# Row transposes of a fused two-block kernel, each split over two 64-row tiles of TensorE

## The chip, the cores and the metric

One NeuronCore of a Trainium2 chip runs the whole program; the other cores idle. The metric is the device time of one execution in microseconds (us). Three runs of the kernel before gave 3456.67 us as their median (3455.22 to 3461.14). The profile shown here is that of one more execution.

## The reference, cut to what matters

1024 tokens of width 1024, in float32, go through two transformer blocks. The first block mixes (a gated linear recurrence beside latent attention, merged by sigmoid gates and projected), adds the residual, normalizes and sends each token to 2 of 32 experts. The second block mixes (a chunked linear recurrence with 4 heads beside a pooling branch), normalizes, and sends each token to 8 of 64 experts. An expert computes, on the rows that were routed to it:

```python
def block_ffn(args):
    xb, e = args
    return (jax.nn.silu(xb @ w_gate[e]) * (xb @ w_up[e])) @ w_down[e]
```

xb has 1024 columns, w_gate[e] and w_up[e] are 1024 x 256, w_down[e] is 256 x 1024. The results are scaled by the router's share and summed per token.

## The kernel before, in words

TensorE multiplies a stationary operand, loaded by LDWEIGHTS, by a moving one, and contracts over the partitions. So whatever is to be multiplied along its columns must first lie with these columns on partitions. Rows of tokens are turned for that with `nc.tensor.transpose(out, rows, ident)`: the 128 x 128 piece of rows is the stationary operand, the identity is the moving one (128 columns), and the turned piece lands in PSUM, from where VectorE copies it to SBUF. Eight such pieces (C = 8) turn 128 tokens of 1024 columns. All engines run their own lists of instructions; semaphores order them.

Five places of this kind matter here.

- **experts** (run twice: for 32, then for 64 experts). A step works on two blocks of 64 tokens of up to two different experts at once: the two halves (PART = 64) sit on two column tiles of the array (shape 128*64 in the profile), the first with the weights from `w_gu`/`w_dn` (lines 1894, 1919), the second with the staged copies `st_gu`/`st_dn` (lines 1897, 1922). TensorE's list for step i is: 8 gate-and-up products per half into `gu_ps`; `turn_rows(i + 1)`, the 8 transposes of the next step's rows into `x_ps` (line 1883), whose source takes every 8th column of `xb` (`xb[:, slot, c:D:C]`); `finish(i)`, the down products of step i - 1 into `y_ps`; and the 2 transposes of the hidden values into `h_ps` (line 1906), whose source takes every 2nd column of `hid` (`hid[:, slot, c::FC]`). A float32 product is issued as two instructions over the 512 moving columns, a transpose as one. VectorE copies `x_ps` out (line 1978) and `h_ps` (line 1980), makes `hid` (1976) and stages weights (1964, 1971); ScalarE does Silu (1944) and the scaling of `y_ps` (1950); GpSimd gathers rows and scatters sums by indirect DMA; SyncE's queue loads 3 MB of weights for each expert, into one of 5 slots in the first experts and of 4 in the second, and posts `g_ready`/`d_ready` (lines 1771, 1775) once they have landed.
- **merge** (the first block's merging stage) and **mix_out** (the second mix's output). For each of 8 tiles of 128 tokens TensorE runs an output projection (32 instructions of 512 columns, lines 1176 and 2505, shape 128*128), then the turn of the tile before (`turn`, lines 1154 and 2484, 8 contiguous pieces), then the router's products of the tile before that (`route`, lines 1165 and 2495, shape 128*64).
- **take_sums** (the sums of the first experts): for 8 tiles VectorE adds two halves of the sums (line 1306), TensorE turns the tile (line 1293), VectorE copies it out (line 1302).

Of the kernel before, what the change touches and what calls it, by code (L numbers as in the profile page):

```python
# [25 lines left out]
P = 128  # L26
S = 1024
D = 1024
T = S // P
C = D // P  # L30
BANK = 512
# [13 lines left out]
PART = P // 2  # L45
# [69 lines left out]
def begin(nc, A, G, gain_of, dst, mask_d, wcol, wgate):  # L115

    ph = phase(nc)
    with ph.ctx:
# [101 lines left out]
        @block.vector  # L221
        def _(v):
            d = nc.vector

            def mean(t):
                v.wait_ge(squared, t + 1)
                d.tensor_scalar(ssq[:, t:t + 1], ssq[:, t:t + 1], 1.0 / D, EPS, ALU.mult, ALU.add).then_inc(meaned, 1)

            def take(t):
                v.wait_ge(turned, t + 1)  # L230
                if t == 0:
                    v.wait_ge(vec_ready, 1)
                d.tensor_tensor(dst[:, :, t * P:(t + 1) * P], tp[:, t % 2, :, :],
                                gain_of[:, :, None].to_broadcast([P, C, P]), ALU.mult).then_inc(taken, 1)

            v.wait_ge(vec_t, 1)
            d.tensor_copy(G.vec[:], vps[:, 0:VROWS]).then_inc(vec_ready, 1)
            v.wait_ge(made, 4)
            mean(0)
            for t in range(T):  # L240
                one = slice(t, t + 1)
                if t + 1 < T:
                    mean(t + 1)
                v.wait_ge(rooted, t + 1)
                d.reciprocal(rstd[:, one], rstd[:, one]).then_inc(inverted, 1)
                v.wait_ge(inverted, t + 1)
                if t >= 2:
                    v.wait_ge(turned, t - 1)
                d.tensor_scalar(diag[:, t % 2, :], G.ident[:], rstd[:, one], None, ALU.mult).then_inc(diag_ready, 1)
                if t:  # L250
                    take(t - 1)
            take(T - 1)

def vec(G, name):
# [820 lines left out]
def merge(nc, A, G, rows_d, sum_d, logits, w_gate):  # L1076
# [4 lines left out]
    ph = phase(nc)  # L1081
    HC = C // 2
    with ph.ctx:
# [8 lines left out]
        rows = ph.sb("rows", [P, 2, D])  # L1092
        rstd = ph.sb("rstd", [P, T])

        tp = ps[:, 0, :].rearrange("p (c t) -> p c t", t=P)
        lps = ps[:, 1, 0:T * W_ROUTE].rearrange("p (t n) -> p t n", n=W_ROUTE)
        (wr_in, gain_in, squared, mean, rooted, rows_ready, turned, cols_ready, routed, row_out0, row_out1,
         sum_out) = ph.sems(
# [36 lines left out]
        def _(pe):  # L1135
# [13 lines left out]
            def turn(t):  # L1149
                pe.wait_ge(rows_ready, t + 1)  # L1150
                if t:
                    pe.wait_ge(cols_ready, t)
                for c in range(C):
                    last = nc.tensor.transpose(tp[:, c, :], rows[:, t % 2, c * P:(c + 1) * P], G.ident[:])
                last.then_inc(turned, 1)

            def route(t):
# [47 lines left out]
        def _(v):  # L1205
# [7 lines left out]

            def take(t):
                v.wait_ge(turned, t + 1)
                d.tensor_copy(G.ya[:, :, t * P:(t + 1) * P], tp).then_inc(cols_ready, 1)

            v.wait_ge(x_in, 16)
            v.wait_ge(gain_in, 16)
# [43 lines left out]
def take_sums(nc, A, G, sum_d, rows, cols):  # L1263

    ph = phase(nc)
    with ph.ctx:
        other = ph.sb("other", [P, T, D])
        tp = ph.ps("tp", [P, 2, C, P])
        turned, taken, added = ph.sems("turned taken added")
        row_in = ph.sems(" ".join(f"row_in{t}" for t in range(T)))  # L1270
        block = ph.ctx.enter_context(nc.Block())
# [14 lines left out]
        @block.tensor  # L1286
        def _(pe):
            for t in range(T):
                pe.wait_ge(added, t + 1)
                if t >= 2:  # L1290
                    pe.wait_ge(taken, t - 1)
                for c in range(C):
                    last = nc.tensor.transpose(tp[:, t % 2, c, :], rows[:, t, c * P:(c + 1) * P], G.ident[:])
                last.then_inc(turned, 1)

        @block.vector
        def _(v):
            d = nc.vector

            def take(t):  # L1300
                v.wait_ge(turned, t + 1)
                d.tensor_copy(cols[:, :, t * P:(t + 1) * P], tp[:, t % 2]).then_inc(taken, 1)

            for t in range(T):
                v.wait_ge(row_in[t], 32)
                d.tensor_tensor(rows[:, t, :], rows[:, t, :], other[:, t, :], ALU.add).then_inc(added, 1)
                if t:
                    take(t - 1)
            take(T - 1)
# [409 lines left out]
def experts(nc, G, E, NB, W, rows_d, sum_d, loaded, stage, work, then=()):  # L1719
# [6 lines left out]
    with ph.ctx:  # L1726
# [13 lines left out]
        st_dn = work[:, 0:FC * D].rearrange("p (c n) -> p c n", c=FC)  # L1740
        x_t = work[:, 2 * D:4 * D].rearrange("p (s c n) -> p s c n", s=2, c=C)
        y = work[:, 4 * D:6 * D].rearrange("p (s n) -> p s n", s=2)
        x_ps = ph.ps("x_ps", [P, C, P])
        gu_ps = ph.ps("gu_ps", [P, 2, 2, F_EXP])
        h_ps = ph.ps("h_ps", [P, BANK // P, P])[:, 0:FC, :]
        y_ps = ph.ps("y_ps", [P, D])
        (g_ready, d_ready, g_staged, d_staged, idx_ready, idx_y_ready, x_turned, x_ready, gu_ready,
         silu_done, hid_ready, h_turned, h_ready, y_ready, share_in, share_ready, y_taken, y_out0, y_out1) = ph.sems(
            "g_ready d_ready g_staged d_staged idx_ready idx_y_ready x_turned x_ready gu_ready "
            "silu_done hid_ready h_turned h_ready y_ready share_in share_ready y_taken y_out0 y_out1")  # L1750
        x_in, y_out = G.xb_in, [y_out0, y_out1]
        PAIRS = (NB + 1) // 2
        block = ph.ctx.enter_context(nc.Block())
# [125 lines left out]
        def _(pe):  # L1879
            def turn_rows(b, slot, landed):  # L1880
                pe.wait_ge(x_in[slot], landed)
                for c in range(C):
                    last = nc.tensor.transpose(x_ps[:, c, :], xb[:, slot, c:D:C], G.ident[:])  # L1883
                last.then_inc(x_turned, 1)

            def step(i, slot, rounds):
# [15 lines left out]
                if not first:  # L1902
                    finish(i)
                pe.wait_ge(hid_ready, i + 1)
                for c in range(FC):
                    last = nc.tensor.transpose(h_ps[:, c, :], hid[:, slot, c::FC], G.ident[:])  # L1906
                last.then_inc(h_turned, 1)

            def finish(i):
# [46 lines left out]
        def _(v):  # L1956
# [17 lines left out]
            def step(i, slot, rounds):  # L1974
                v.wait_ge(silu_done, i + 1)
                d.tensor_tensor(hid[:, slot, :], act_g[:, slot, :], gu_ps[:, slot, 1, :], ALU.mult).then_inc(hid_ready, 1)  # L1976
                v.wait_ge(x_turned, i + 2)
                d.tensor_copy(x_t[:, 1 - slot], x_ps[:]).then_inc(x_ready, 1)  # L1978
                v.wait_ge(h_turned, i + 1)
                d.tensor_copy(hid_t[:], h_ps).then_inc(h_ready, 1)  # L1980
                v.wait_ge(share_in, i + 1)
                d.tensor_copy(share[PART:P, slot:slot + 1], share_b[PART:P, slot:slot + 1]).then_inc(share_ready, 1)
                stage_down(i)
                stage_gate_up(i + 2, slot)

            stage_gate_up(0, 0)
            v.wait_ge(x_turned, 1)
            d.tensor_copy(x_t[:, 0], x_ps[:]).then_inc(x_ready, 1)  # L1988
            stage_gate_up(1, 1)
            steps(v, step)  # L1990

# [453 lines left out]
def mix_out(nc, A, G, rows_d, logits, w_out):  # L2445
# [3 lines left out]
    with ph.ctx:  # L2449
# [5 lines left out]
        var = ph.sb("var", [P, T])  # L2455
        shift = ph.sb("shift", [P, T])
        ps = ph.ps("ps", [P, 2, D])
        tp = ph.ps("tp", [P, C, P])
        lps = ph.ps("lps", [P, T, E2])
        (wr_in, vec_in, ready, summed_in, summed, mean, squared, var_ready, rooted, rstd_ready, dve, normed,  # L2460
         rows_ready, stored, turned, cols_ready, routed) = ph.sems(
# [16 lines left out]
        def _(pe):  # L2478
            def turn(t):
# [1 line left out]
                if t:  # L2481
                    pe.wait_ge(cols_ready, t)
                for c in range(C):
                    last = nc.tensor.transpose(tp[:, c, :], G.h[:, t, c * P:(c + 1) * P], G.ident[:])
                last.then_inc(turned, 1)

            def route(t):
# [44 lines left out]
        def _(v):  # L2532
# [2 lines left out]

            def take(t):
                v.wait_ge(turned, t + 1)
                d.tensor_copy(G.u[:, :, t * P:(t + 1) * P], tp[:]).then_inc(cols_ready, 1)

            v.wait_ge(vec_in, 32)  # L2540
            for t in range(T):
# [294 lines left out]
```

## Time and profile before

| | |
|---|---|
| median of 3 runs | 3456.67 us |
| the profiled execution, its time | 3455.7 us |
| its span from first to last instruction | 3454.0 us |
| TensorE busy with matmuls | 3156.8 us, 91% |
| mean granted TensorE clock | 0.957 of full speed |
| first experts, first and last turn of rows | 1397.4 and 1718.0 us |
| second experts, first and last turn of rows | 2416.0 and 3377.2 us |

The profile gives times from the span's start. PE is TensorE's matmul side and PEld its weight-load side; the two overlap, and a matmul's recorded duration includes its way through the array, so that matmuls which follow each other overlap in the record. What one costs is therefore read from the distance between starts. "1.0" of the granted clock is 2.4 GHz, "0.5" is 1.2 GHz.

### The profile page before, as it was taken

Reading aid. Unit: us, or ns where it says so; the run is one execution under the profiler, and the core shown is the slowest. Engines: PE = TensorE matmul, PEld = TensorE weight load, DVE = VectorE, ACT = ScalarE, POOL = GpSimd, SP = SyncE. Lnnn points to the kernel's source line nnn. Section 1 sums busy time; section 2 is a strip of 40 time slices with the busy share of each in tenths; the row PEclk is TensorE's granted clock in tenths of the full one; section 3 lists DMA queues with packets and bytes.
Section 4 is the critical chain, followed back from the end, with each engine's and each line's share of the span. In section 5 each row is a group of like instructions: output and inputs, shape, how many; then the busy total and the mean of one; then the engine's idle time right before and its main releaser. Section 6 shows DMA issues by size and latency. Waiting matters only on the chain. (4 is left out here: it accounts for less than half of the span.)

```text
span 3454.0 us, 46196 instructions
## 1 busy us (share of the span) xinstructions
PE 3156.8 (91%) x14927; PEld 1544.3 (45%) x14928; DVE 1567.1 (45%) x2431; ACT 727.7 (21%) x1169; POOL 703.4 (20%) x917
## 2 busy tenths in 40 slices
PE   8999989987999996789969998988999999999992
PEld 4444445544665444333337773444333333333330
DVE  3322234446775123434456675344444444444444
ACT  2222223343543001011123330211011111111112
POOL 1000000000000000334510000000455545555552
PEclk9999999998999997899979998999999999999996
DMA  6201021124231124799740111221888998898885
GB/s 230 98 30 43 0 85 50 54 68 95 52 96 50 30 112 195 270 386 384 267 156 25 34 30 49 83 95 65 305 273 274 350 331 293 292 300 277 272 263 181
DMA packets 180326, 564.84 MB, mean 164 GB/s; under 512 B 18684, under 2 KB 93024, under 8 KB 143072
## 3 DMA queue, kind: packets, MB, share of 16 engines
q1 hardware_dynamic: 142864, 429.69, 32.9%
q0 software_dynamic: 34128, 127.45, 15.0%
q10 hardware_dynamic: 3240, 6.45, 0.5%
q8 instruction: 59, 0.97, 0.1%
q14 instruction: 35, 0.29, 0.0%
HBM read 460.27 MB, written 103.27 MB: 163 GB/s over the span
## 5 line engine op out<-in xcount | busy, mean ns | idle before, releaser
L1894 PE MATMUL gu_ps<-w_gu,second 128*64 x1648 | 741.2, 603 | 13.8 <-DVE second L1988 8.6
L1897 PE MATMUL gu_ps<-h,second 128*64 128x512 f32 x1648 | 741.2, 603 | 0.0
L1894 PEld LDWEIGHTS gu_ps<-w_gu,second 128*64 128x64 f32 x1648 | 220.1, 139 | 448.1 <-issue 436.5
L1919 PE MATMUL y_ps<-w_dn,hid_t 128*64 x824 | 379.1, 603 | 11.6 <-issue 8.7
L1922 PE MATMUL y_ps<-second,hid_t 128*64 128x512 f32 x824 | 379.1, 603 | 0.0
L1522 POOL COPY moe_idx<-moe_slot_tok 128x1 int32<-128x1 int32 x4 | 0.6, 183 | 1811.0 <-DVEq L1457 1225.0
L355 PE MATMUL front<-second,wcol 128*128 128x512 f32 x768 | 332.1, 595 | 4.8 <-ACTq L63 2.4
L1964 DVE COPY h<-w_gu 128x4096 f32 x109 | 249.6, 2290 | 96.2 <-SPq L1771 96.0
L1848 POOL DMA_INDIRECT token_sums<-second,idx_y x103 | 243.3, 2362 | 18.0 <-issue 16.9
L355 PEld LDWEIGHTS front<-second,wcol 128*128 128x128 f32 x768 | 146.4, 191 | 189.6 <-issue 189.6
L1897 PEld LDWEIGHTS gu_ps<-h,second 128*64 128x64 f32 x1648 | 220.1, 139 | 0.0
L1950 ACT ACTIVATE second<-y_ps,share 128x1024 f32<-128x1024 f32 x103 | 114.7, 1113 | 461.4 <-PE y_ps L1922 461.4
L1919 PEld LDWEIGHTS y_ps<-w_dn,hid_t 128*64 128x64 f32 x824 | 105.2, 138 | 203.3 <-issue 191.6
L1944 ACT ACTIVATE act_g<-gu_ps 128x256 f32<-128x256 f32 x105 | 40.2, 383 | 728.7 <-PE gu_ps L1897 723.0
L1843 POOL TENSOR_TENSOR idx_y<-moe_slot_tok,moe_side 128x1 int32<-128x1 int32 x103 | 81.2, 788 | 530.0 <-ACT second L1950 530.0
L1976 DVE TENSOR_TENSOR hid<-act_g,gu_ps 128x256 f32<-128x256 f32 x105 | 44.1, 420 | 282.2 <-ACT act_g L1944 282.1
L1980 DVE COPY hid_t<-h_ps 128x256 f32<-128x256 f32 x105 | 44.5, 424 | 279.0 <-PE h_ps L1906 271.1
L1971 DVE COPY second<-w_dn 128x2048 f32 x105 | 128.9, 1227 | 52.5 <-issue 52.3
L1883 PEld LDWEIGHTS x_ps<-ident,moe_xb 128*128 128x128 f32 x840 | 102.5, 193 | 104.7 <-issue 93.0
L1847 POOL TENSOR_TENSOR mark_y<-tok 128x1 f32<-128x1 f32 x103 | 143.3, 1391 | 21.9 <-DMA token_sums<-second,idx_y 11.4
L1883 PE MATMUL x_ps<-ident,moe_xb 128*128 128x128 f32 x840 | 122.9, 290 | 20.1 <-PEq L95 19.9
L1978 DVE COPY second<-x_ps 128x1024 f32<-128x1024 f32 x105 | 128.5, 1224 | 23.3 <-PE x_ps L1883 23.3
(453 smaller groups left out, 4780.1 us busy)
## 6 DMA issues: line engine op xcount, KB each, us to landing
w_gu<-in_w_gate_dram SPq DMA_DIRECT2D x96, 1024.0 KB, 12.8
w_gu<-in_w_up_dram SPq DMA_DIRECT2D x96, 1024.0 KB, 15.8
w_dn<-in_w_down_dram SPq DMA_DIRECT2D x96, 1024.0 KB, 10.5
wcol<-in_w_in_dram SPq DMA_DIRECT2D x12, 1024.0 KB, 5.4
qk_by_head<-stage SPq DMA_DIRECT2D x32, 384.0 KB, 3.7
qk<-qk_by_head SPq DMA_DIRECT2D x16, 768.0 KB
w_gu<-in_w_in_dram SPq DMA_DIRECT2D x20, 512.0 KB, 5.0
token_sums<-zero POOLq DMA_DIRECT2D x19, 512.0 KB, 12.6
```

Of the source, the lines that this page charges most:

```text
L355: last = nc.tensor.matmul(ps[:, slot, c, h * BANK:(h + 1) * BANK], wcol[:, k, kc, c * P:(c + 1) * P], G.u[:, kc, h * BANK:(h + 1) * BANK], ...
L1847: g.tensor_tensor(mark_y[:, slot:slot + 1], G.tok[:, 0:1], G.tok[:, 0:1], ALU.add).then_inc(idx_y_ready, 1)
L1848: g.indirect_dma_start(sum_d, bass.IndirectOffsetOnAxis(ap=idx_y[:, slot:slot + 1], axis=0), y[:, slot, :], None, compute_op=ALU.add).then ...
L1883: last = nc.tensor.transpose(x_ps[:, c, :], xb[:, slot, c:D:C], G.ident[:])
L1894: nc.tensor.matmul(gu_ps[0:PART, slot], x_t[:, slot, c, 0:PART], w_gu[:, bass.ds(ws, 1), :, c, :].rearrange("p o g n -> p (o g) n"), start ...
L1897: last = nc.tensor.matmul(gu_ps[PART:P, slot], x_t[:, slot, c, PART:P], st_gu[:, slot, :, c, :], start=c == 0, stop=c == C - 1)
L1919: nc.tensor.matmul(y_ps[0:PART, cs], hid_t[:, c, 0:PART], w_dn[:, bass.ds(ws, 1), c, cs].rearrange("p o n -> p (o n)"), start=c == 0, stop ...
L1922: last = nc.tensor.matmul(y_ps[PART:P, cs], hid_t[:, c, PART:P], st_dn[:, c, cs], start=c == 0, stop=c == FC - 1)
L1950: s.activation(y[:, 1 - slot, :], y_ps[:], ACT.Copy, scale=share[:, 1 - slot:2 - slot]).then_inc(y_taken, 1)
L1964: d.tensor_copy(st_gu[:, slot].rearrange("p g c n -> p (g c n)"), w_gu[:, bass.ds(e % W, 1)].rearrange("p o g c n -> p (o g c n)")).then_i ...
L1971: d.tensor_copy(st_dn.rearrange("p c n -> p (c n)"), w_dn[:, bass.ds(e % W, 1)].rearrange("p o c n -> p (o c n)")).then_inc(d_staged, 1)
L1978: d.tensor_copy(x_t[:, 1 - slot], x_ps[:]).then_inc(x_ready, 1)
```

## The change

A new helper turns a 128 x 128 piece in two instructions. The first takes the partitions 0 to 63 (64 tokens) as the stationary operand, with the identity's 64 x 64 corner as the moving one, the second the partitions 64 to 127 (shape 64*128 where the profile names tiles). Each writes 64 columns on all 128 partitions. The output tiles get an outer dimension of two (`a`), so that the two halves of a tile lie in different PSUM banks; `h_ps` grows from part of one bank to parts of two. The copies out of PSUM read and write in that order of dimensions, over the same number of elements. In the experts a post on a new semaphore, `turn_go`, stands between each wait and the transposes that it holds back. Nothing waits on `turn_go`. The transposes of the other stages are left as they were.

```diff
@@ -250,6 +250,14 @@
             take(T - 1)
+
+
+def turn_rows_by_half(nc, G, out, src):
+
+    for a in range(2):
+        rows = slice(a * PART, (a + 1) * PART)
+        last = nc.tensor.transpose(out[:, a], src[rows, :], G.ident[rows, rows])
+    return last
@@ -1092,7 +1100,7 @@
 
-        tp = ps[:, 0, :].rearrange("p (c t) -> p c t", t=P)
+        tp = ps[:, 0, :].rearrange("p (a c t) -> p a c t", a=2, t=PART)
@@ -1151,7 +1159,7 @@
                 for c in range(C):
-                    last = nc.tensor.transpose(tp[:, c, :], rows[:, t % 2, c * P:(c + 1) * P], G.ident[:])
+                    last = turn_rows_by_half(nc, G, tp[:, :, c, :], rows[:, t % 2, c * P:(c + 1) * P])
@@ -1213,7 +1221,7 @@
                 v.wait_ge(turned, t + 1)
-                d.tensor_copy(G.ya[:, :, t * P:(t + 1) * P], tp).then_inc(cols_ready, 1)
+                d.tensor_copy(G.ya[:, :, t * P:(t + 1) * P].rearrange("p c (a n) -> p a c n", a=2), tp).then_inc(cols_ready, 1)
@@ -1265,7 +1273,7 @@
         other = ph.sb("other", [P, T, D])
-        tp = ph.ps("tp", [P, 2, C, P])
+        tp = ph.ps("tp", [P, 2, 2, C, PART])
@@ -1290,7 +1298,7 @@
                 for c in range(C):
-                    last = nc.tensor.transpose(tp[:, t % 2, c, :], rows[:, t, c * P:(c + 1) * P], G.ident[:])
+                    last = turn_rows_by_half(nc, G, tp[:, t % 2, :, c, :], rows[:, t, c * P:(c + 1) * P])
@@ -1299,7 +1307,7 @@
                 v.wait_ge(turned, t + 1)
-                d.tensor_copy(cols[:, :, t * P:(t + 1) * P], tp[:, t % 2]).then_inc(taken, 1)
+                d.tensor_copy(cols[:, :, t * P:(t + 1) * P].rearrange("p c (a n) -> p a c n", a=2), tp[:, t % 2]).then_inc(taken, 1)
@@ -1740,14 +1748,14 @@
         y = work[:, 4 * D:6 * D].rearrange("p (s n) -> p s n", s=2)
-        x_ps = ph.ps("x_ps", [P, C, P])
+        x_ps = ph.ps("x_ps", [P, 2, C, PART])
         gu_ps = ph.ps("gu_ps", [P, 2, 2, F_EXP])
-        h_ps = ph.ps("h_ps", [P, BANK // P, P])[:, 0:FC, :]
+        h_ps = ph.ps("h_ps", [P, 2, BANK])[:, :, 0:FC * PART].rearrange("p a (c n) -> p a c n", c=FC)
...
         (g_ready, d_ready, g_staged, d_staged, idx_ready, idx_y_ready, x_turned, x_ready, gu_ready,
-         silu_done, hid_ready, h_turned, h_ready, y_ready, share_in, share_ready, y_taken, y_out0, y_out1) = ph.sems(
+         silu_done, hid_ready, h_turned, h_ready, y_ready, share_in, share_ready, y_taken, y_out0, y_out1, turn_go) = ph.sems(
             "g_ready d_ready g_staged d_staged idx_ready idx_y_ready x_turned x_ready gu_ready "
-            "silu_done hid_ready h_turned h_ready y_ready share_in share_ready y_taken y_out0 y_out1")
+            "silu_done hid_ready h_turned h_ready y_ready share_in share_ready y_taken y_out0 y_out1 turn_go")
@@ -1879,8 +1887,9 @@
                 pe.wait_ge(x_in[slot], landed)
+                pe.sem_inc(turn_go, 1)
                 for c in range(C):
-                    last = nc.tensor.transpose(x_ps[:, c, :], xb[:, slot, c:D:C], G.ident[:])
+                    last = turn_rows_by_half(nc, G, x_ps[:, :, c, :], xb[:, slot, c:D:C])
@@ -1902,8 +1911,9 @@
                 pe.wait_ge(hid_ready, i + 1)
+                pe.sem_inc(turn_go, 1)
                 for c in range(FC):
-                    last = nc.tensor.transpose(h_ps[:, c, :], hid[:, slot, c::FC], G.ident[:])
+                    last = turn_rows_by_half(nc, G, h_ps[:, :, c, :], hid[:, slot, c::FC])
@@ -1975,9 +1985,9 @@
                 v.wait_ge(x_turned, i + 2)
-                d.tensor_copy(x_t[:, 1 - slot], x_ps[:]).then_inc(x_ready, 1)
+                d.tensor_copy(x_t[:, 1 - slot].rearrange("p c (a n) -> p a c n", a=2), x_ps[:]).then_inc(x_ready, 1)
                 v.wait_ge(h_turned, i + 1)
-                d.tensor_copy(hid_t[:], h_ps).then_inc(h_ready, 1)
+                d.tensor_copy(hid_t[:].rearrange("p c (a n) -> p a c n", a=2), h_ps).then_inc(h_ready, 1)
@@ -1985,7 +1995,7 @@
             v.wait_ge(x_turned, 1)
-            d.tensor_copy(x_t[:, 0], x_ps[:]).then_inc(x_ready, 1)
+            d.tensor_copy(x_t[:, 0].rearrange("p c (a n) -> p a c n", a=2), x_ps[:]).then_inc(x_ready, 1)
@@ -2455,7 +2465,7 @@
         ps = ph.ps("ps", [P, 2, D])
-        tp = ph.ps("tp", [P, C, P])
+        tp = ph.ps("tp", [P, 2, C, PART])
@@ -2481,7 +2491,7 @@
                 for c in range(C):
-                    last = nc.tensor.transpose(tp[:, c, :], G.h[:, t, c * P:(c + 1) * P], G.ident[:])
+                    last = turn_rows_by_half(nc, G, tp[:, :, c, :], G.h[:, t, c * P:(c + 1) * P])
@@ -2535,7 +2545,7 @@
                 v.wait_ge(turned, t + 1)
-                d.tensor_copy(G.u[:, :, t * P:(t + 1) * P], tp[:]).then_inc(cols_ready, 1)
+                d.tensor_copy(G.u[:, :, t * P:(t + 1) * P].rearrange("p c (a n) -> p a c n", a=2), tp[:]).then_inc(cols_ready, 1)
```

## Rows read from the trace of the kernel before

**Rows 1.** The page: busy time of the engines, clock, DMA.

```profile
...
PE 3156.8 (91%) x14927; PEld 1544.3 (45%) x14928; DVE 1567.1 (45%) x2431; ACT 727.7 (21%) x1169; POOL 703.4 (20%) x917
...
PEclk9999999998999997899979998999999999999996
DMA  6201021124231124799740111221888998898885
...
```

**Rows 2.** Stretches of experts and the two mixing stages; columns as its second line says.

```profile
...
core 0: us, PE busy (x) PEld busy (x) DVE busy (x) ACT busy (x) POOL busy (x), PEclk, DMA share, GB/s
1410.00:1750.00 340.00, 295.74 (x1370) 109.80 (x1366) 140.98 (x150) 36.32 (x49) 145.70 (x192) 0.94 0.90 327
2440.00:3380.00 940.00, 939.73 (x4500) 352.71 (x4498) 436.66 (x464) 115.60 (x155) 498.82 (x616) 1.00 0.88 290
1238.00:1345.00 107.00, 101.91 (x515) 53.21 (x513) 29.03 (x37) 9.47 (x21) 0.00 (x0) 0.97 0.17 69
2186.00:2298.00 112.00, 102.35 (x516) 53.23 (x514) 39.84 (x58) 26.82 (x42) 0.00 (x0) 0.97 0.08 33
...
```

**Rows 3.** Who waited, window 1410 to 1750: line, releaser, total us, times, longest.

```profile
...
DVE h L1964 <- SPq L1771: 73.1, 13, 14.8
...
```

**Rows 4.** Second experts, line 1883: durations ns min/median/max, first and last start.

```profile
...
L1883 PEld LDWEIGHTS x_ps<-ident,moe_xb x640: 185/192/231, 2416.0 to 3377.2; 128*128 128x128 f32 x160
L1883 PE MATMUL x_ps<-ident,moe_xb x640: 272/275/451, 2416.0 to 3377.3; 128*128 128x128 f32 x160
...
```

**Rows 5.** Second experts, line 1906, the same columns.

```profile
...
L1906 PE MATMUL h_ps<-ident,hid x158: 281/336/387, 2433.9 to 3381.3; 128*128 128x128 f32 x158
...
```

**Rows 6.** Line 1883 in the first experts.

```profile
...
L1883 PE MATMUL x_ps<-ident,moe_xb x200: 272/276/451, 1397.4 to 1718.1; 128*128 128x128 f32 x100
...
```

**Rows 7.** One step on TensorE, in order of time: start us, us, instructions merged.

```profile
...
2599.63 0.59 PE L1897 MATMUL gu_ps<-h,second 128*64 128x512 f32 x1
2600.16 1.15 PE L1883 MATMUL x_ps<-ident,moe_xb 128*128 128x128 f32 x8
2601.24 0.64 PE L1919 MATMUL y_ps<-w_dn,hid_t 128*64 x1
2601.25 0.64 PE L1922 MATMUL y_ps<-second,hid_t 128*64 128x512 f32 x1
2601.72 0.59 PE L1919 MATMUL y_ps<-w_dn,hid_t 128*64 x1
...
2604.30 0.59 PE L1922 MATMUL y_ps<-second,hid_t 128*64 128x512 f32 x1
2604.83 0.50 PE L1906 MATMUL h_ps<-ident,hid 128*128 128x128 f32 x2
2605.26 0.64 PE L1894 MATMUL gu_ps<-w_gu,second 128*64 x1
...
```

**Rows 8.** The next step, TensorE.

```profile
...
2612.28 1.15 PE L1883 MATMUL x_ps<-ident,moe_xb 128*128 128x128 f32 x8
...
```

**Rows 9.** The first transpose of a step alone.

```profile
...
2600.16 0.38 PE L1883 MATMUL x_ps<-ident,moe_xb 128*128 128x128 f32 x1
```

**Rows 10.** VectorE in the same step: start us, us, [idle before, releaser].

```profile
...
2601.35 1.23 DVE L1978 COPY second<-x_ps 128x1024 f32<-128x1024 f32 x1 [0.24 <-PE x_ps L1883]
2605.37 0.42 DVE L1980 COPY hid_t<-h_ps 128x256 f32<-128x256 f32 x1 [2.79 <-PE h_ps L1906]
...
```

**Rows 11.** Contiguous pieces turned at full clock, line 2484: durations ns min/median/max.

```profile
...
L2484 PEld LDWEIGHTS tp<-ident,second x64: 139/141/230, 2186.7 to 2294.3; 128*128 128x128 f32 x64
L2484 PE MATMUL tp<-ident,second x64: 272/273/476, 2187.2 to 2294.5; 128*128 128x128 f32 x64
...
```

**Rows 12.** mix_out on TensorE: projection, turn, route, projection.

```profile
...
2200.91 1.02 PE L2505 MATMUL ps<-w_gu,w_dn 128*128 128x512 f32 x2
2201.77 1.04 PE L2484 MATMUL tp<-ident,second 128*128 128x128 f32 x8
2202.74 1.15 PE L2495 MATMUL lps<-w_route,h 128*64 128x64 f32 x32
2203.82 0.70 PE L2505 MATMUL ps<-w_gu,w_dn 128*128 128x512 f32 x1
```

**Rows 13.** The route of merge, 36 moving columns, on TensorE.

```profile
...
1254.30 1.13 PE L1165 MATMUL ps<-w_route,h 128*64 128x36 f32 x32
1255.36 0.70 PE L1176 MATMUL ps_o<-w_out,h 128*128 128x512 f32 x1
```

**Rows 14.** take_sums: last tile.

```profile
...
1771.26 1.73 PE L1293 MATMUL tp<-ident,second 128*128 128x128 f32 x8 [0.55 <-DVE second L1306]
1773.03 1.23 DVE L1302 COPY h<-tp 128x1024 f32<-128x1024 f32 x1 [0.69 <-PE tp L1293]
...
```

**Rows 15.** SyncE queue of the second experts: start us, us of the issue.

```profile
...
2600.42 0.33 SPq L1695 DMA_DIRECT2D w_gu<-in_w_gate_dram  x1
...
2612.66 0.34 SPq L1695 DMA_DIRECT2D w_gu<-in_w_gate_dram  x1
...
```

**Rows 16.** The page, DMA issues: KB each, median us from issue to landing.

```profile
...
w_gu<-in_w_up_dram SPq DMA_DIRECT2D x96, 1024.0 KB, 15.8
...
```

## The prediction

> **What bounds the kernel now.** I read the page first: TensorE is busy for 91% of the span, VectorE for 45% [rows 1]. An average over stages says little, so next come the stretches [rows 2]. In the second experts TensorE is busy for 939.7 of 940 us at full clock; in merge and mix_out for 102 of 107 and 102 of 112 us. The first experts are another case: TensorE is busy for 296 of 340 us with the DMA engines at 0.90, and VectorE waited 73 us for weights to land, in 13 waits, up to 14.8 us [rows 3]. There the weights set the pace.
>
> Then one step of the second experts in order of time [rows 7]. It lasts 12.12 us (2600.16 to 2612.28) [rows 7, 8]. Pairs of products on the two column tiles start every 0.43 us. The turn of rows takes 2600.16 to 2601.24, so 1.08 us; the hidden transposes and the way to the next products 2604.83 to 2605.26, 0.43 us. Nothing is waited for at either place: VectorE's copies start after them (2601.35, 2605.37) and end microseconds before TensorE wants their result [rows 10]. So every nanosecond that a turn gives back in the second experts shortens the span, 80 turns of rows (640 transposes) and 79 of hidden values (158) [rows 4, 5].
>
> **What sets the pace inside a turn.** This decides the case. A transpose needs a load of 128 stationary columns and then a pass of the moving identity, and loads run under the passes of the piece before.
>
> - The pass. 512 moving columns take 0.43 us [rows 7], so 128 take 0.107 and 64 take 0.053.
> - The load. The first matmul of a turn has nothing in front of it and its record holds the load too: 0.38 us alone against a median of 0.275, so a strided load (every 8th column) takes 0.105 [rows 4, 9]. In the hidden turn (every 2nd column) the first is 387 ns against 281, 0.106 again [rows 5]. A load of 64 columns for a product takes 0.64 - 0.59 = 0.05 [rows 7].
> - Contiguous pieces load faster: 141 ns recorded against 192 for the strided ones of equal size [rows 4, 11], so 0.105 - 0.05 = about 0.055.
>
> In the strided turn the distance of transposes is (1.15 - 0.275 - 0.105) / 7 = 0.110 us [rows 4, 7], in the contiguous one (1.04 - 0.273) / 7 = 0.110 [rows 11, 12]. The first is held by load and pass alike (0.105 and 0.107), the second by the pass alone.
>
> Halving the moving columns halves the pass and leaves the load at 128 columns. The trace has no row tiles, but it has pairs on column tiles with short passes, which are nearest: route runs 16 pairs of 64-column loads and 64-column passes at (1.15 - 0.222 - 0.05) / 15 = 0.058 us (0.222 is the record of a pass of 64 columns: the 0.275 of 128 columns less 0.053) [rows 12], and route in merge, with 36 columns instead of 64, is no faster: 1.13 us for the same 32 instructions [rows 13]. So two tiles do load and pass side by side, and once passes are short the load is the bound, plus some 5 ns.
>
> **The sum, part by part.**
>
> *Experts, turn of rows.* 16 transposes in 8 pairs. Distance of pairs: the load, 0.105 + 0.005 = 0.110, what it is now. Only the last pass ends 0.053 earlier, less some 0.005 for the start of the second tile (0.01 apart at most) [rows 7]: -0.05 us. *Hidden turn:* the same, -0.05. Entering and leaving costs nothing new: the shape already changes from 128*64 to 128*128 and back, and takes 0.53 - 0.43 = 0.10 us each time (2604.30 to 2604.83) [rows 7]; I take the same for 64*128. Bound below for the change of shape: a shallower tile empties earlier, by at most half of this, 0.05; above, twice the value, +0.10. 159 turns x 0.05 = -8.0 us.
>
> *First experts.* 25 and 24 turns [rows 6]. What TensorE saves there is handed to the wait for weights [rows 3]; only after the last stall it counts: -0.2, and at most 49 x 0.05 = 2.5.
>
> *merge and mix_out.* Now the turn is in the same shape as the projection before it, and from its first pass to route's first load it takes 2201.77 to 2202.74, 0.97 us [rows 12]. After: change of shape 0.10, first load 0.055, 7 distances of 0.06, last pass 0.053, change of shape 0.10: 0.73, so -0.24. Eight turns, and one turn per stage that is followed by a projection rather than by route pays 0.2 more for a way back that was free: -1.8 per stage, -3.6 for both, and both stages are bound by TensorE [rows 2].
>
> *take_sums.* Seven of 8 turns lie under VectorE's adds and copies; at the last VectorE waited 0.69 us [rows 14]. The passes there are partly at half clock; I take half of the 1.73 us less its way through: -0.5.
>
> *Copies out of PSUM* move the same elements; if their new order made them a tenth slower, it would be 0.12 us under the slack named above. *The post on turn_go* and the 10 more loads and 10 more passes in a step: in route 64 instructions go out in 1.1 us, 17 ns each [rows 12], while TensorE gets about 120 in a step of 12.12 us. Nothing. *Faster steps* ask for weights 1% sooner: their issues follow at a step's distance and land after 15.8 us at the median, more than a step before use with four slots [rows 15, 16]. Nothing.
>
> Sum: -8.0 - 0.2 - 3.6 - 0.5 = -12.3 us. The profiled execution took 3455.7 us, of which 3454.0 are the span; it lies 1.0 under the median. 3456.7 - 12.3 = 3444 us.
>
> **A rule that speaks against it.** Here the contiguous load was recorded at 141 ns and the strided one at 192 [rows 4, 11]. The Trainium skill, "TensorE: Matmul & The Clock Gate", section "LDWEIGHTS (loading the stationary operand)", states that a load costs its number of columns at 1.2 per ns whatever the contraction, so 107 ns for 128 columns on half as many rows. For the strided loads this and the trace agree (0.105), and it says that a split pays nothing inside a turn. For contiguous ones the trace differs, and by the rule the two mixing stages would lose instead of gaining.
>
> **Rivals.**
>
> 1. *Contiguous loads lose their speed on row tiles* and take 0.105 like the others. A turn in the mixing stages is then 0.10 + 0.105 + 7 x 0.11 + 0.053 + 0.10 = 1.13, +0.16 instead of -0.24: with the one way back 16 x 0.16 + 0.4 = +3.0 instead of -3.6. Time 3444 + 6.6 = 3451. For it: the fast load shows only on whole 128 x 128 pieces [rows 11]. Against: nothing in the trace ties it to them. 0.10. (By the rule above of the Trainium skill, "TensorE: Matmul & The Clock Gate", it would come out so; no run here shows a load on half the rows.)
> 2. *Strided loads get faster too* when each fetches half the rows, towards the 0.055 of contiguous ones. Then distances fall by up to 0.05: a step gains 0.10 + 7 x 0.05 + 0.05 = 0.5 us, 79 steps 40 us; half of it is nearer. Time 3405 to 3430. For it: a speed tied to access is seen to vary by two [rows 4, 11]. Against: each partition still yields the same 128 strided values. 0.14.
> 3. *Row tiles don't pass side by side*, since both write all 128 partitions of PSUM, where column tiles write 64 each. Two passes of 0.053 are the old one; the experts give nothing, the mixing stages pay their changes of shape, 16 x 0.16 + 0.4 = +3. Time 3459. For it: the trace has only column pairs. Against: two banks. 0.13.
> 4. *Loads of the two row tiles go one after the other.* Each pair costs 0.21 in place of 0.11: +0.8 for rows, +0.2 for hidden values, 1.0 us a step, 79 us, some 10 more in the first experts and the mixing stages. Time about 3545. It is slower from the point where the second load adds over 0.015 us to a pair (159 turns hold 79 x 10 pairs; 12 + 7 us over 790). Against: the column tiles' loads start 0.01 apart [rows 7]. 0.11.
> 5. *Each change into or out of the new shape, or the post, costs more* than 0.12 us a turn: 159 x 0.12 = 19 us takes the gain back and 7 us more. At +0.10 to +0.20 the time is 3460 to 3476. 0.08.
>
> The forecast itself has 0.44, with a range of its own of 3434 to 3450 (changes of shape down to 0.05 cheaper, or a little dearer).
>
> **Numbers.** 0.2% is 7 us, about what a measurement of this kernel can tell from no change, so faster means under 3449.8 and slower over 3463.6. Faster: 0.43 of the forecast, all of 2, a little of 1: 0.58. Same: nearly all of 1 and 3, a little of 5: 0.24. Slower: 4 and most of 5: 0.18. For the range, 4 is left out above with part of 5, and the lower third of 2 below: 3417 to 3464.
>
> **What the profile would show.** Steps of 12.02 us instead of 12.12; from the first load of a turn to the next product 1.03 instead of 1.08 us, with pairs 0.11 apart; in mix_out 0.73 instead of 0.97 us from the end of the projection's last pass to route's first load, with pairs 0.06 apart; loads of 141 and 192 ns as before. A distance of 0.21 proves rival 4, of 0.06 in the experts rival 2, of 0.11 in mix_out rivals 1 (long loads) or 3 (short ones); a longer gap ahead of the first load proves 5. The prediction goes wrong above all if the load of a row tile isn't what it is for the whole array.

## The result: slower by 2.75%

| | before | after |
|---|---|---|
| median | 3455.94 us (4 runs) | 3551.51 us (4 runs, 3547.85 to 3555.02) |
| ratio, 95% interval | | 1.0275 [1.0257, 1.0293] |
| span of the profiled execution | 3454.0 us | 3553.3 us |
| first to last turn of rows in the second experts | 961.2 us [rows 4] | 1064.6 us |

The forecast was 3444 us, the range 3417 to 3464; the time lies 88 us above the range. The span grew by 99.3 us. The second experts' turns reach over 103.4 us more. Everything ahead of their first turn got faster, by 5.7 us (2410.3 instead of 2416.0), and 1.6 us were lost behind their last. The page and the stretch of the second experts after the change:

```profile
PE 3164.4 (89%) x16165; PEld 1542.7 (43%) x16166; DVE 1567.3 (44%) x2431; ACT 728.0 (20%) x1169; POOL 700.9 (20%) x917
...
PEclk9999999989999995999799999999999999999996
```

```profile
core 0: us, PE busy (x) PEld busy (x) DVE busy (x) ACT busy (x) POOL busy (x), PEclk, DMA share, GB/s
2440.00:3480.00 1040.00, 958.71 (x5246) 359.62 (x5242) 435.18 (x462) 115.53 (x155) 497.42 (x616) 0.97 0.81 262
```

TensorE was busy in 939.7 of 940 us before [rows 2]; now it has 81 us of idle time there, and its granted clock is 0.97 of the full one instead of 1.00, so it spends part of the stretch at the lower level. Where the gap is, one step shows, in order of time on TensorE:

```profile
2903.80 0.59 PE L1903 MATMUL gu_ps<-w_gu,second 128*64 x1
...
2904.32 1.10 PE L259 MATMUL x_ps<-ident,moe_xb 64*128 64x64 f32 x16
2906.32 0.64 PE L1929 MATMUL y_ps<-w_dn,hid_t 128*64 x1 [0.90 <-issue]
...
2909.37 0.59 PE L1929 MATMUL y_ps<-w_dn,hid_t 128*64 x1
```

Line 259 is in the new helper; lines 1929 and 1903 are those of the down and of the gate products of the first half. The 16 transposes together take 1.10 us, 0.05 less than the 8 whole ones [rows 7]. Then the array stands still for 0.90 us, and not for another engine: "issue" says that TensorE's own list had not got there. Compare the turns' and the down products' starts: 2.00 us apart now, 1.08 before.

In mix_out, by contrast, the turn does what was forecast:

```profile
2230.48 0.59 PE L2515 MATMUL ps<-w_gu,w_dn 128*128 128x512 f32 x1
2231.00 0.71 PE L259 MATMUL tp<-ident,second 64*128 64x64 f32 x16
2231.64 1.15 PE L2505 MATMUL lps<-w_route,h 128*64 128x64 f32 x32
```

From the end of the projection's last pass (2230.48 + 0.43) to route's first load it is 0.73 us, where it was 0.97 [rows 12].

**What TensorE's list does meanwhile.** Beside loads and matmuls, TensorE's list holds waits and register work. The profile shows that work as PEldq, and it can run long before the array is done with the matmuls that stand ahead of it on the list: these must then be waiting in some queue. (The queue itself is seen in no trace; it is my reading of the times below.) `finish` begins with such work: it loads the expert's number from SBUF into a register (TENSOR_LOAD, line 1910 before, 1920 after), which chooses the weights' slot. The same load over the second experts, before and then after (ns min/median/max, first and last start):

```profile
L1910 PEldq TENSOR_LOAD <-moe_blk_e x79: 297/302/964, 2439.9 to 3388.3; - x79
```

```profile
L1920 PEldq TENSOR_LOAD <-moe_blk_e x79: 298/1061/1635, 2436.1 to 3487.4; - x79
```

And in single steps, the one of [rows 7], whose turn starts at 2600.16, and the one shown above, whose turn starts at 2904.32:

```profile
L1910 PEldq TENSOR_LOAD <-moe_blk_e x1: 302/302/302, 2597.6 to 2597.6; - x1
```

```profile
L1920 PEldq TENSOR_LOAD <-moe_blk_e x1: 1067/1067/1067, 2904.4 to 2904.4; - x1
```

Before, the load ran 2.6 us ahead of the turn and lasted 0.3 us. After, it starts 0.1 us behind the turn's start, lasts 1.07 us, and the first down product follows 0.80 us after its end (2905.5 to 2906.3); the rest of `finish`'s waits and register work lies between. Over the second experts the median start moved from 1.8 us ahead of the turn to 0.13 us behind it. So two things happened: the list lost its run-ahead, and the load that now lies in the open takes three to five times as long.

### The profile page after: what moved, and what is told of

It is laid out like the page before. It is cut to its first block and busy times, and to the rows that moved or that the text cites. A ratio compares the mean times of both kernels' runs of the same rounds, so it can differ in the third digit from the quotient of the medians.

```text
span 3553.3 us, 48880 instructions
## 1 busy us (share of the span) xinstructions
PE 3164.4 (89%) x16165; PEld 1542.7 (43%) x16166; DVE 1567.3 (44%) x2431; ACT 728.0 (20%) x1169; POOL 700.9 (20%) x917
## 5 line engine op out<-in xcount | busy, mean ns | idle before, releaser
L1929 PE MATMUL y_ps<-w_dn,hid_t 128*64 x824 | 406.0, 639 | 98.6 <-issue 93.9
L1932 PE MATMUL y_ps<-second,hid_t 128*64 128x512 f32 x824 | 406.5, 640 | 0.0
L259 PEld LDWEIGHTS x_ps<-ident,moe_xb 64*128 64x128 f32 x1680 | 101.0, 200 | 104.9 <-issue 104.9
L2140 PE MATMUL proj_ps<-h,w_gu 128*128 128x512 f32 x288 | 134.2, 609 | 2.2 <-PEq L95 2.0
```

Of the source, the lines that this page charges most:

```text
L1929: nc.tensor.matmul(y_ps[0:PART, cs], hid_t[:, c, 0:PART], w_dn[:, bass.ds(ws, 1), c, cs].rearrange("p o n -> p (o n)"), start=c == 0, stop ...
L1932: last = nc.tensor.matmul(y_ps[PART:P, cs], hid_t[:, c, PART:P], st_dn[:, c, cs], start=c == 0, stop=c == FC - 1)
L2140: last = nc.tensor.matmul(big[:, slot, half * BANK:(half + 1) * BANK], w[:, n, kc, :], G.u[:, kc, half * BANK:(half + 1) * BANK], start=kc ...
```

## Experiments

The theory at the start: 32 instructions of a turn (16 loads, 16 passes) instead of 16 fill TensorE's queue, so that the list stands until the turn begins. The expert's number then comes too late for the down products. The rivals: the post on `turn_go` holds TensorE back; the split transposes, or the loads of the two row tiles, are slow by themselves. "Before" in each comparison is the kernel before on the same chip.

### The register load ahead of the turn

```diff
+                if not first:
+                    e_done = pe.value_load(G.blk_e[0:1, 0, bass.ds(i - 1, 1)], min_val=0, max_val=E - 1)
                 turn_rows(i + 1, 1 - slot, 16 if first else rounds + 32)
                 if not first:
-                    finish(i)
+                    finish(i, e_done)
...
```

(`finish` takes the number as an argument instead of loading it.)

> The changed kernel with one edit: in a step of the experts the load of the expert number into a register that the down products need stands ahead of the turn of rows on TensorE's list, instead of behind it. Theory (run-ahead lost): the 32 instructions of the split turn fill TensorE's queue, so that this load starts only when the turn does, lasts 1.0 to 1.6 us there instead of 0.3, and the down products wait for it. Moved ahead it is done in time: steps of the second experts fall from 12.98 at the median to about 11.98 (12.12 less 0.10 in the rows' turn and 0.05 in the hidden one), second experts 80 x 11.98 = 950 instead of 1064 us, time about 3440 us. Rival A (the post on turn_go holds TensorE back): the post is still there, no gain, 3552. Rival B (the split transposes are themselves slower): 3552.

Measured: 3444.14 us, ratio 0.9957 [0.994, 0.9973]; in a second set of runs, below, 3441.38 us. The load takes 301 ns at the median. The step:

```profile
2847.58 1.10 PE L259 MATMUL x_ps<-ident,moe_xb 64*128 64x64 f32 x16
2848.61 0.64 PE L1930 MATMUL y_ps<-w_dn,hid_t 128*64 x1
...
2852.19 0.45 PE L259 MATMUL h_ps<-ident,hid 64*128 64x64 f32 x4
2852.57 0.64 PE L1903 MATMUL gu_ps<-w_gu,second 128*64 x1
```

```profile
2859.59 1.10 PE L259 MATMUL x_ps<-ident,moe_xb 64*128 64x64 f32 x16
```

The turn to the first down product is 1.03 us instead of 1.08, the hidden turn to the next product 0.38 instead of 0.43 [rows 7], and a step 12.01. The whole loss is gone, and with it both rivals: the post and all split transposes are still there. The control puts the same move into the kernel before:

> Control: the kernel before with the same move of the register load ahead of the turn of rows, all transposes whole. Theory (run-ahead lost): the load was early enough already but in the few steps whose rows came late, so 3455 us, steps of 12.12. If the move by itself were worth much (the down products of the kernel before waited for their register now and then), it would be 3450 or less.

Measured: 3455.91 us, ratio 0.9994 [0.9984, 1.0004]. The move alone is worth nothing that can be measured. It repairs what the split turn breaks.

### Which of the split turns it is

The changed kernel with the rows' turn whole:

```diff
-                pe.sem_inc(turn_go, 1)
                 for c in range(C):
-                    last = turn_rows_by_half(nc, G, x_ps[:, :, c, :], xb[:, slot, c:D:C])
+                    last = nc.tensor.transpose(x_ps[:, c, :], xb[:, slot, c:D:C], G.ident[:])
...
```

(`x_ps` and the copies out of it are as before, too.)

> The changed kernel, but the turn of rows in the experts as before (8 whole transposes, no post there); hidden turn, merging stages and the sums split as in the change. Theory (run-ahead lost): 16 instructions leave the queue room, the register load is early again; steps of 12.12 - 0.05 = 12.07, time 3456 - 6 (stages ahead of the second experts, as in the changed kernel) - 4 = about 3446 us. Rival A (a post costs): one of two posts is left, so half the loss, about 3500. Rival B (split transposes slow): 4 of 20 split instructions are left in a step, about 3475.

Measured: 3444.85 us (3442.75 to 3455.7, 5 runs), ratio 0.9974 [0.9956, 0.9991]; steps of 12.07 at the median. The kernel before with only the rows' turn split (the same edit the other way round):

> The kernel before with only the turn of rows in the experts split (with its post); hidden turn, merging stages and the sums whole. Theory (run-ahead lost): the whole loss of the second experts stands, steps near 13.0 at the median and 13.3 in the mean, time 3455 + 105 = about 3560 us. Rival A (each post costs the same): about 3510.

Measured: 3565.41 us, ratio 1.0307 [1.0289, 1.0324]. The rows' turn carries all of the loss; the other four split turns together carry a gain. The posts alone, in the kernel before:

```diff
                 pe.wait_ge(x_in[slot], landed)
+                pe.sem_inc(turn_go, 1)
...
                 pe.wait_ge(hid_ready, i + 1)
+                pe.sem_inc(turn_go, 1)
```

> The kernel before, all transposes whole, with nothing added but the two posts on turn_go in a step of the experts. Theory (run-ahead lost, by the number of instructions of the turn): no difference, 3456 us within 4. If the post itself held TensorE back, or if a wait carried by a post instead of by a load cost the run-ahead, time goes up by a share of the 100 us, at least to 3480.

Measured: 3458.88 us, ratio 1.0006 [0.9996, 1.0015]. The two posts cost nothing that can be measured.

### Count or shape

If the count of instructions is what fills the queue, whole transposes must do it too:

```diff
-                for c in range(C):
+                for c in [*range(C), *range(C)]:
                     last = nc.tensor.transpose(x_ps[:, c, :], xb[:, slot, c:D:C], G.ident[:])
```

> The kernel before, in which the 8 whole transposes of the rows' turn are issued twice into the same places: 32 instructions without any row tile and without a post. Theory (the queue fills by count): the register load of the down products starts some 0.1 us after the turn does, as in the changed kernel, instead of 1.8 before it, and lasts 1.0 us or more at the median. The array alone needs 8 x 0.11 = 0.88 us more, steps of 13.0; the down products can start once the load is done and 0.77 later, 2.0 to 2.5 us after the turn's start against 1.97 for the array, so steps of 13.1 to 13.3 and a time of 3535 to 3550. If row tiles or the change of shape hold the list back and not the count, the load starts 1.8 us ahead, lasts 0.3, and steps are 13.0, time 3526.

Measured: 3549.33 us (2 runs), ratio 1.0265 [1.0247, 1.0284], within the count's forecast. The step and its register load:

```profile
2907.47 2.05 PE L1883 MATMUL x_ps<-ident,moe_xb 128*128 128x128 f32 x16
2909.50 0.64 PE L1919 MATMUL y_ps<-w_dn,hid_t 128*64 x1
```

```profile
L1910 PEldq TENSOR_LOAD <-moe_blk_e x1: 1094/1094/1094, 2907.6 to 2907.6; - x1
```

No row tile and no post, and the load again starts 0.1 us behind the turn; over all steps its median is 1097 ns. So neither the row tiles nor the post is needed to lose the run-ahead: the longer list of the same whole transposes does it.

Next, 24 and 28 instructions instead of 32: the first 4 or 6 pieces split, the rest whole.

```diff
                 for c in range(C):
-                    last = turn_rows_by_half(nc, G, x_ps[:, :, c, :], xb[:, slot, c:D:C])
+                    if c < SPLIT:
+                        turn_rows_by_half(nc, G, x_half[:, :, c, :], xb[:, slot, c:D:C])
+                    else:
+                        b2, at = divmod(c - SPLIT, WHOLE)
+                        last = nc.tensor.transpose(x_whole[:, b2, at, :], xb[:, slot, c:D:C], G.ident[:])
...
```

> The changed kernel, but of the 8 pieces of the rows' turn 4 are split and 4 whole: 24 instructions instead of 32 (16 before); VectorE copies the result out in two instructions. Theory (a queue that fills): 24 leave room for some run-ahead, the register load starts ahead of SyncE's issues, takes 0.3 us, and nothing is lost: 3446 to 3452 us. If each split piece cost its share, half the loss would stand: about 3500.

Measured: 3454.77 us, ratio 0.9995 [0.9985, 1.0004].

> The same with 6 pieces split and 2 whole: 28 instructions. In the changed kernel TensorE's list went on past the turn when 28 instructions of it were still waiting. By that the register load starts just before the turn, some 0.4 us ahead of where it starts in the changed kernel, and SyncE's issues, which begin 0.26 us into the turn, miss most of it: under a third of the loss, 3450 to 3480 us. If each split piece cost its share: about 3527.

Measured: 3453.58 us, ratio 0.9997 [0.9987, 1.0006]. In these two the register load takes 302 and 301 ns at the median and starts 1.35 and 1.33 us ahead of the turn, so a run-ahead is kept even with 28 instructions. I had expected it to be nearly gone there. With the whole turn's 16 instructions it is 1.8 us: it shrinks a little from 16 to 24, not from 24 to 28, and is gone at 32. The time with 4 pieces split lies 3 us over its forecast, and the time with 6 pieces inside its own, though for another reason than the one given: a turn that changes shape in its middle takes 1.22 us to the first down product, against 1.03 when all pieces are split, some 16 us over 79 steps.

```profile
2852.01 0.66 PE L259 MATMUL x_ps<-ident,moe_xb 64*128 64x64 f32 x8
2852.59 0.71 PE L1900 MATMUL x_ps<-ident,moe_xb 128*128 128x128 f32 x4
2853.23 0.64 PE L1937 MATMUL y_ps<-w_dn,hid_t 128*64 x1
```

### Why the register load is slow where it now lies

In the changed kernel SyncE issues the next weights just then, on the same signal that ends the gate products. So the weights later:

```diff
-                sp.wait_ge(gu_ready, blocks_to(e))
+                seen = blocks_to(e)
+                sp.wait_ge(gu_ready, seen)
+                sp.wait_ge(h_turned, seen)
                 load_gate_up(sp, G, e, u)
```

> The changed kernel, the register load left behind the turn, but SyncE issues a step's loads of gate and up weights some 5 us later (it waits for the hidden turn of the same step as well). Theory, second half (the register load of 0.3 us lasts 1.0 to 1.6 because SyncE's two DMA issues run just then): its median falls back to 0.3 us, it still starts with the turn, and steps become those of the few in the changed kernel where the issues came late, 12.24 us; second experts 968 instead of 1064 us, time about 3457. If the load is slow because transposes run or because the queue is full, its median stays at 1.0 and the time at 3550.

Measured: 3490.3 us, ratio 1.0096 [1.0079, 1.0112], the load at 432 ns at the median but up to 1591. Neither answer: about two thirds of the loss went, the rest stayed. The trace of the changed kernel says more. In 18 of its 79 steps no issue of SyncE's overlaps a load that is slow all the same, at a median of 1.00 us. So it isn't SyncE's issuing. What else lies there is seen in the DMA queues. For 3.5 us from the turn's start on, in the kernel before (q0 carries GpSimd's gathers and scatters, q1 the weights):

```profile
q0 software_dynamic: 130, 0.48, 84.0%
q1 hardware_dynamic: 12, 0.10, 11.5%
```

That is the adding scatter of the previous rows into the sums, 4 KB packets (in the changed kernel, 2904.4 to 2907.8, q0 has 83.8% as well). Where the load used to run (2597.6 to 2597.9) no packet is in flight. With the weights later (a turn at 2868.10) it is the other way round:

```profile
q1 hardware_dynamic: 174, 1.29, 87.9%
q0 software_dynamic: 24, 0.10, 14.0%
```

So the DMA engines are as full, but with weights, and the load is quick in most steps. The single loads can be sorted by the packets that run beside them. In the changed kernel 73 of 79 have the scatter's beside them and last 0.80 to 1.64 us; 5 have weights alone and last 0.30 to 0.36 us. With the weights later 20 have the scatter's (0.91 to 1.59 us) and 58 weights alone (median 0.35, but up to 1.14 us). It was the scatter, then, that I suspected, and I took its addition away (this leaves the summation of the experts' rows out):

```diff
                 g.indirect_dma_start(sum_d, bass.IndirectOffsetOnAxis(ap=idx_y[:, slot:slot + 1], axis=0),
-                                     y[:, slot, :], None, compute_op=ALU.add).then_inc(y_out[slot], 16)
+                                     y[:, slot, :], None).then_inc(y_out[slot], 16)
```

> The changed kernel, but GpSimd writes the experts' rows to the sums instead of adding them there (the last writer of a row stands; this leaves the summation out). In the changed kernel the slow register loads run while the 4 KB packets of the adding scatter occupy the DMA engines (they begin with the turn and last 3.5 us; with weights issued later they move, and the load falls to 0.43 us at the median). Theory: the adding scatter makes the load slow. Then its median falls to 0.3 - 0.5 us and the time towards 3460. If a plain scatter delays it as much, or it is slow for another reason, the median stays near 1.0 and the time near 3550.

> Control to the plain scatter: the kernel before with it (the summation left out in the same way). TensorE sets the pace and its register loads run ahead, so the second experts keep steps of 12.12 us; 3455 us, a few less at most from the end of either experts phase.

Measured: 3450.95 us, ratio 0.9984 [0.9975, 0.9994], with the split turn; 3431.72 us, ratio 0.9925 [0.9907, 0.9943], without. The control (2 runs) missed its forecast: it gained 25 us where a few were expected, in the profiled execution all of it ahead of the second experts (their first turn at 2393.1 instead of 2416.0). Most of that is the first experts, where weights set the pace: there (1410 to 1740) q0's packets take 65 us of each DMA engine's time instead of 97. So only the difference of the two counts: 19 us are left of about 97. The load's median fell from 1061 to 532 ns, its longest from 1635 to 581.

So the adding scatter's traffic makes the load slow, by up to five times. The plain one's slows it by less than two, but that is not the same place: with plain writes the burst of packets lasts 1.4 us instead of 3.5 and the load falls 0.75 to 1 us behind its start, with the addition 0.1 to 0.6 us. The run doesn't separate the kind of the traffic from its length and place. The place does matter: a second register load on the list, of the next block's expert number for the gate products, runs 1.5 us behind the turn's start, still inside the adding scatter, and takes 0.59 us at the median, against 0.31 with plain writes (the kernel before, then the control):

```profile
L1888 PEldq TENSOR_LOAD <-moe_blk_e x78: 302/587/840, 2433.9 to 3365.7; - x78
```

```profile
L1888 PEldq TENSOR_LOAD <-moe_blk_e x76: 297/306/338, 2432.9 to 3341.8; - x76
```

### The version that beats both

> The version with the register load ahead of the split turn once more, for a closer ratio to the kernel before: 0.9962 within 0.001, 3444 us.

Measured: 3441.38 us (3439.39 to 3446.1, 5 runs), ratio 0.9954 [0.9941, 0.9968] to the kernel before: split turns everywhere, and the register load ahead of the rows' turn.

## Why the prediction was wrong

- **The step that failed** reads: "The post on turn_go and the 10 more loads and 10 more passes in a step: in route 64 instructions go out in 1.1 us, 17 ns each [rows 12], while TensorE gets about 120 in a step of 12.12 us. Nothing." It counted the rate at which the list hands instructions over, and not what stands behind them on the list: the register work of `finish`, which the prediction never names. No run contradicts the rate. But with 32 instructions in the rows' turn the list goes on past them only once the turn has begun, 0.02 us after its start, where it was 1.9 us ahead with 16, and everything behind is late by that. Of the items in the sentence, the posts were free (e5_posts_only), the 2 loads and 2 passes more for the hidden turn were free (e3_rows_whole), and the 8 and 8 more for the rows' turn cost some 105 us (e4_rows_only).
- **The cover that went.** The same step had to name what hides the register work of `finish`, and the trace of before had the answer: TENSOR_LOAD, at a median of 302 ns, mostly one to 2.6 us ahead of the turn. It now starts 0.13 us into the turn, and even a quick one leaves 0.13 + 0.30 + 0.81 = 1.24 us to the first down product, where the turn needs 1.03. Five steps of the changed kernel in a row show this, from 2843.1 on, in which the load took 0.30 to 0.36 us: 1.23 to 1.29 us. So the lost run-ahead alone costs 0.2 us a step, some 16 us in all. The load's own slowness, 1.06 us at the median and 1.5 or more in 31 of 79 steps, makes the rest. From the turn to the first down product it is 2.14 us in the mean, against 1.03 with the load moved: 87 us in all.
- **The clock took a further part.** The granted clock of the stretch is 0.97; with the load moved ahead it is 1.00. In 16 steps the clock falls to the lower level for a few us, each time less than 1 us after the array has stood still for 1.3 to 1.5 us; 15 steps with such a pause keep the full clock. One step of each kind, from turn to turn, in the columns of [rows 2]:

```profile
2570.20:2583.70 13.50, 12.14 (x72) 4.62 (x70) 5.65 (x6) 1.50 (x2) 6.54 (x8) 1.00 0.32 78
2596.60:2611.70 15.10, 13.75 (x70) 5.01 (x68) 5.65 (x6) 1.50 (x2) 6.46 (x7) 0.89 0.27 67
```

  Steps with the fall take 15.1 to 15.3 us, the 15 others 13.4 to 13.6: 16 x 1.7 = 27 us. With the 87 us of the item above this makes 114, about the 112 us that separate the changed kernel's second experts from those of e1_load_early (1064.6 against 952.9 us).
- **What was right.** Inside a turn each part came out as summed. Strided pairs start 0.11 us apart (0.111 at the median, from the starts in the trace). The turn to the next product takes 1.03 us, the hidden one 0.38. Contiguous pairs are 0.06 apart, with 0.73 us in mix_out. The loads are recorded at 202 ns (strided) and 139 ns (contiguous); 192 and 141 were forecast. Steps are 12.01 with the load moved, 12.02 forecast; the time is 3441 to 3444, forecast 3444. But that is the time of another kernel. What lay ahead of the second experts gained 5.7 us, against 4.3 forecast; with the load moved 3.9 and 5.7 us, so this is known to some 2 us.
- **Slips in its sums.** Eight turns at -0.24 and one way back of 0.2 are -1.7 a stage, not -1.8. Rival 4 would make the kernel slower from (12 + 7) / 790 = 0.024 us a pair on, not 0.015. Neither decides anything.
- **The rule on loads.** On row tiles strided pairs follow at 0.11 us and contiguous ones at 0.06. The rule of the Trainium skill, "TensorE: Matmul & The Clock Gate", section "LDWEIGHTS (loading the stationary operand)", that was weighed in the prediction, 107 ns for 128 columns, agrees with the first and not with the second. Rival 1, fast loads lost on row tiles, is out.
- **Rival 4 had the time and not the cause.** It priced loads that go one after the other at 3545. The page of the changed kernel might seem to agree; the step doesn't: 16 transposes in 1.10 us are side by side. Its own test, a distance of 0.21 between pairs, is what tells a right price from a right reason. Rivals 2 and 3 are out by the same distances. Rival 5 is out as well: in mix_out route starts 0.15 us after the last transposes do, which is their pass of 0.05 and the 0.10 taken for the change of shape. In the experts the down products start 0.20 us after them; there either the pass waits 0.05 us for its load or leaving costs 0.05 more, and both are in the 1.03 us. Nor did any sign in the prediction's last paragraph point at a gap behind a turn.

What stays open is the form of the limit. A turn of 28 instructions keeps a run-ahead of 1.3 us, one of 32 has none, and no run tells what makes that step; that it is the room of a queue is the reading that fits, and is not shown. Why the adding scatter slows the load of one number into a register was not tried further.

## What to carry to other kernels

Before an edit multiplies the matmuls of a burst, look at the register loads, branches and waits that stand behind the burst on TensorE's own list: they are done early only as long as the list gets past the burst in time, which here it did with 28 instructions and not with 32. Put such work ahead of the burst, where it cost nothing in this kernel (e2_load_early_whole), and read an "issue" idle ahead of a matmul as a question to the list, not to the array. Splitting a transpose over two row tiles halves the pass but not the load: it pays for contiguous pieces (0.24 us of 0.97 in a turn of 128 x 1024) and hardly for strided ones (0.05 of 1.08).

## What the runs showed of the hardware that was not expected

- A register load on TensorE takes 0.30 us with no packet in flight, mostly under 0.5 us beside weights alone, 0.31 to 0.58 us beside a plain scatter, and 0.8 to 1.6 us in the first part of an adding scatter; 1.5 us into one it is 0.59 us at the median.
- The run-ahead of TensorE's list past a turn, by the start of the register load, is 1.8 us at the median with 16 instructions in the turn, 1.3 with 24 and with 28, and gone with 32: then the list goes on 0.02 us after the turn has begun.
- On row tiles too the pace of a transpose goes by its source's stride: pairs of contiguous pieces follow at 0.06 us (loads recorded at 139 ns), pairs of every eighth column at 0.11 us (202 ns).
- Pauses of 1.3 to 1.5 us in an array that is otherwise busy were followed by a fall of the granted clock in 16 of 31 cases, at 1.7 us a fall.
